# Gated recurrence of a two-layer block: outputs with tokens on partitions, chunk matmuls in column groups, norm along the free axis, scan between the state updates, one table set for exp and ln

## What is computed

```python
f = lb + (1.0 - lb) * jax.nn.sigmoid(f_x)
q = heads(jax.nn.silu(q_x)); k = heads(1.0 - f); log_f = heads(jnp.log(f)); v = heads(i_x)
b = jnp.cumsum(log_f, axis=3)                       # inside a chunk
q_rel = q * jnp.exp(b - b_ref); k_rel = k * jnp.exp(b_ref - b)
a = jnp.where(causal, q_rel @ k_rel.T, 0.0); o_intra = a @ v
q_dec = q * jnp.exp(b); k_dec = k * jnp.exp(b_last - b)
o_inter = q_dec @ state                             # per chunk
state = exp(b_last)[..., None] * state + k_dec.T @ v
o = rms_norm(o_intra + o_inter, o_norm) * silu(g_x) # norm over the 128 values
return o @ w_o
```

## Time and profile before

| | us |
|---|---|
| median of 3 runs | 1766.31 |
| lowest, highest | 1765.16, 1770.31 |
| span of the profiled execution, first to last instruction | 1764.1 |
| median less that span | 2.2 |
| recurrence, from the first score matmul of head 0 to that of head 7 | 1103.60 to 1312.89 |

### The profile page before, as it was taken

How to read it: one execution, slowest core, us unless ns; L and a number is a source line. 1 busy time by engine, 2 the same in 40 slices (tenths; PEclk the granted TensorE clock), 3 DMA queues, 4 the chain that set the end, 5 groups by cost and what they waited for, 6 DMA issues and landing times.

```text
span 1764.1 us, 28709 instructions
## 1 busy us (share of the span) xinstructions
PE 1648.9 (93%) x10394; PEld 1339.2 (76%) x10394; DVE 843.9 (48%) x1461; ACT 750.5 (43%) x1160; POOL 647.9 (37%) x374
## 2 busy tenths in 40 slices
PE   5999989988889999999999999899999999999996
PEld 4787668856666668878888887788878878888885
DVE  6555768856765645522121245565663532111125
ACT  2333334343744445524142347676764622223231
POOL 4454310004421125634444454233334544444440
PEclk9999999989899999999999999899999999999997
DMA  8622210003111123232333332122222223333331
GB/s 287 203 84 72 72 37 4 4 18 86 53 48 34 30 70 84 84 95 84 104 88 106 91 101 60 48 61 70 71 77 82 57 85 95 96 94 99 92 104 52
DMA packets 250959, 140.35 MB, mean 80 GB/s; under 512 B 10121, under 2 KB 242656, under 8 KB 250864
## 3 DMA queue, kind: packets, MB, share of 16 engines
q1 hardware_dynamic: 249552, 137.12, 26.7%
q0 software_dynamic: 1008, 1.66, 0.3%
q10 hardware_dynamic: 304, 0.26, 0.0%
HBM read 136.93 MB, written 2.10 MB: 79 GB/s over the span
## 4 chain that ended last, share of the span: by engine, by line
issue 40%; PE 24%; POOL 11%; DVE 11%; ACT 5%; DVEq 4%; DMA 2%; ACTq 1%; POOLq 1%; SPq 1%
PE bank L746 13%; POOL w_low L555 10%; DVE hg_state L2062 2%; DVE bank L2059 2%; PE bank L797 2%; PE bank L1035 1%; DVEq L2489 1%; DMA x_tok<-in_x 1%; DVE hg_k_dec L2059 1%; PE bank L1197 1%; PE bank L1196 1%; PE bank L1224 1%; DVEq L2802 1%; SPq L439 1%; ACTq L2008 1%
## 5 line engine op out<-in xcount | busy, mean ns | idle before, releaser
L555 POOL TENSOR_TENSOR w_low<-w_raw,w_high 128x1024 fp32r<-128x1024 f32 (+2 forms) x218 | 516.6, 2370 | 971.5 <-ACT w_high L1486 971.4
L746 PE MATMUL bank<-act_high,w_high 128*128 128x512 f32 x976 | 391.5, 401 | 12.3 <-POOL w_low L555 8.3
L746 PE MATMUL bank<-act_low,w_high 128*128 128x512 f32 x976 | 382.4, 392 | 0.0
L746 PE MATMUL bank<-act_high,w_low 128*128 128x512 f32 x976 | 382.2, 392 | 0.0
L1486 ACT ACTIVATE w_high<-w_raw 128x1024 fp32r<-128x1024 f32 (+2 forms) x218 | 219.1, 1006 | 282.2 <-PE bank L746 269.7
L746 PEld LDWEIGHTS bank<-act_high,w_high 128*128 128x128 f32 x976 | 184.0, 189 | 65.3 <-issue 12.2
L746 PEld LDWEIGHTS bank<-act_high,w_low 128*128 128x128 f32 x976 | 184.0, 189 | 40.1
L746 PEld LDWEIGHTS bank<-act_low,w_high 128*128 128x128 f32 x976 | 183.9, 188 | 38.8 <-issue 2.4
L746 PE MATMUL bank<-hid_high,w_high 128*128 128x512 f32 x472 | 185.1, 392 | 3.8 <-DVE mix_out L2731 3.8
L746 PE MATMUL bank<-hid_low,w_high 128*128 128x512 f32 x472 | 184.4, 391 | 0.0
L746 PE MATMUL bank<-hid_high,w_low 128*128 128x512 f32 x472 | 184.2, 390 | 0.0
(11 more groups left out here) (568 smaller groups left out, 2855.4 us busy)
## 6 DMA issues: line engine op xcount, KB each, us to landing
w_raw<-in_mlp_w SPq DMA_DIRECT2D x128, 512.0 KB, 4.0
w_raw<-in_hgrn_w_in SPq DMA_DIRECT2D x32, 512.0 KB, 4.1
w_raw<-in_w_in SPq DMA_DIRECT2D x29, 512.0 KB, 4.0
w_ada_piece<-in_w_ada SPq DMA_DIRECT2D x5, 2048.0 KB, 16.4
w_raw<-in_w_out SPq DMA_DIRECT2D x8, 512.0 KB, 3.9
w_raw<-in_mla_w_o SPq DMA_DIRECT2D x8, 512.0 KB, 3.9
w_raw<-in_hgrn_w_o SPq DMA_DIRECT2D x8, 512.0 KB, 3.9
w_raw<-in_mla_w_in SPq DMA_DIRECT2D x6, 512.0 KB, 4.0
```

Of the source, the lines that this page charges most:

```text
L555: gp.tensor_tensor(WL[:, c0 % 2, 0:kt, 0:m], WR[:, c0 % 2, 0:kt, 0:m], WH[:, c0 % 2, 0:kt, 0:m].bitcast(F32), ALU.subtract).then_inc(w_lo, 1)
L746: mm = pe.matmul(bank[0:m, :], w[:, k, 0:m], a[:, k0 + k, :], start=(k == 0 and n_ == 0), stop=(k == kt - 1 and n_ == 2))
```

## The change

PE makes the outputs with tokens on partitions: for each block of 128 tokens the masked scores are the weights and the values move (one full 128x128 matmul), and each chunk's 32 columns of q_dec are weights of one column group of the array, with its state moving, so that four chunks go to four groups of 32 output partitions. The sum of squares by a matmul is gone: ACT squares each 128x128 block with a sum along the free axis, takes Ln and Exp of 128x4 numbers, DVE scales each token's row and PE turns the result back (`turn_outputs`). The outputs stand after job G0+2 instead of before it (in the second call, after block 4 of job G0+3). DVE makes three state updates, then the scan, the differences and `scaled(1)`, then the other twelve. On ACT the gate's Silu moves beside that of q, one table set for exp and ln is loaded by hand, and q_dec's and the decay's exponential come behind the norm, ahead of `high(G0+4)`. The q_dec product waits for a semaphore of its own (`g_dec`).

```diff
@@ tensor
+                    else:
+                        pe.wait_ge(g_fin, o)
                     for c_ in range(NC - 1):
 ...
+                def outputs():
+                    pe.wait_ge(g_qdec, o + 1)
                     for t in range(TT):
-                        pe.matmul(PB[6][:, t * P:(t + 1) * P], VG[:, t, :], AT[:, t, :], start=True, stop=False)
+                        pe.matmul(PB[6][:, t * P:(t + 1) * P], AT[:, t, :], VG[:, t, :], start=(t == 0), stop=False)
                         for b in range(P // HC):
                             c_ = t * (P // HC) + b
                             if c_:
                                 pe.wait_ge(g_st, o * (NC - 1) + c_)
-                                mm = pe.matmul(PB[6][:, c_ * HC:(c_ + 1) * HC], ST[:, c_, :],
-                                               QDEC[:, c_ * HC:(c_ + 1) * HC], start=False,
+                                mm = pe.matmul(PB[6][b * HC:(b + 1) * HC, t * P:(t + 1) * P],
+                                               QDEC[:, c_ * HC:(c_ + 1) * HC], ST[:, c_, :], start=False,
 ...
-                def square_sum():
-                    pe.wait_ge(g_sq, o + 1)
-                    pe.matmul(PB[7][:, :], ONES[:, :], OSQ[:, :], start=True, stop=True).then_inc(g_ss, 1)
+                def turn_outputs():
+                    pe.wait_ge(g_scaled, o + 1)
+                    for t in range(TT):
+                        mm = pe.transpose(PB[5][:, t * P:(t + 1) * P], OTK[:, t, :], IDENT[:, :])
+                    mm.then_inc(g_back, 1)
                 if second:
-                    job(G0 + 3, n * 4, free["g"], n * 4 + 4, amid=square_sum)
+                    job(G0 + 3, n * 4, free["g"], n * 4 + 4, amid=outputs, amid_at=4)
+                elif o is not None and n is not None:
+                    job(G0 + 1, n * 4, free["g"], n * 4 + 2)
+                    job(G0 + 2, n * 4, free["g"], n * 4 + 3)
+                    outputs()
+                    job(G0 + 3, n * 4, free["g"], n * 4 + 4)
                 elif o is not None:
+                    part(W0, (free["go"], 1), "hgrn_o", 3, 7, HH, HL)
+                    outputs()
+                    part(W0 + 1, (free["go"], 2), "hgrn_o", 0, 4, HH, HL)
+                if o is not None:
+                    turn_outputs()
+                if n is not None and o is not None:
+                    turn_values(n, o)
@@ scalar
+                if o is not None:
+                    act.wait_ge(free["g"], o * 4 + 6)
+                    act.activation(GG[:, :], TG[3][:, :], ACT.Silu).then_inc(g_gate, 1)
 ...
+                act.preload_act_table_set("natural_log_exp_and_others")
                 if n is not None:
                     act.wait_ge(g_diff, n + 1)
 ...
                     act.activation(KDEC[:, :], TG[0][:, :], ACT.Exp)
+                    act.drain()
+                    act.sem_inc(g_exp, 1)
+                if o is not None:
+                    act.wait_ge(g_out, o + 1)
+                    for t in range(TT):
+                        act.activation(OSQ[:, t * P:(t + 1) * P], PB[6][:, t * P:(t + 1) * P], ACT.Square,
+                                       accum_out=OST[:, 0, t:t + 1])
+                    act.drain()
+                    act.activation(OST[:, 1, :], OST[:, 0, :], ACT.Ln, scale=1.0 / P, bias=CST[:, 3:4])
+                    act.drain()
+                    act.activation(OST[:, 2, :], OST[:, 1, :], ACT.Exp, scale=-0.5).then_inc(g_rstd, 1)
+                if n is not None:
                     act.activation(QDEC[:, :], BG[:, :], ACT.Exp)
 ...
                 if n is not None and o is not None:
                     high(G0 + 4, n * 4)
@@ vector
+                BEFORE = 3
+                if o is not None:
+                    states(0, BEFORE)
                 if n is not None:
                     dve.wait_ge(g_ln, n + 1)
                     dve.tensor_tensor_scan(BG[:, :], HRST[:, :], TG[2][:, :], 0.0, MUL, ADD)
 ...
+                if o is not None:
+                    states(BEFORE, T // HC - 1)
 ...
                 if o is not None:
-                    dve.wait_ge(g_sd, o + 1)
-                    stt(OG[:, :], OG[:, :], col("o_norm"), OSD[:, :], MUL, MUL)
+                    dve.wait_ge(g_rstd, o + 1)
+                    tt(OTK[:, :, :], PB[6][:, :].rearrange("p (t d) -> p t d", d=P), bc(OST[:, 2, :], P), MUL)\
+                        .then_inc(g_scaled, 1)
+                if n is not None:
+                    dve.wait_ge(g_dec, n + 1)
+                    tt(QDEC[:, :], QDEC[:, :], QG[:, :], MUL).then_inc(g_qdec, 1)
+                if o is not None:
                     dve.wait_ge(g_gate, o + 1)
-                    tt(OG[:, :], OG[:, :], GG[:, :], MUL)
+                    if n is not None:
+                        scaled(3, TG[3])
+                    dve.wait_ge(g_back, o + 1)
+                    stt(OG[:, :], PB[5][:, :], col("o_norm"), GG[:, :], MUL, MUL)
                     after(g_fin)
```

More of the change, by code:

```diff
@@ L1396, in hgrn @@
                     mm.then_inc(g_out, 1)
-                if n is not None:
-                    if o is not None and not second:
-                        job(G0 + 2, n * 4, free["g"], n * 4 + 3)
-                else:
-                    part(W0 + 1, (free["go"], 2), "hgrn_o", 0, 2, HH, HL)
-                def square_sum():
-                    pe.wait_ge(g_sq, o + 1)
-                    pe.matmul(PB[7][:, :], ONES[:, :], OSQ[:, :], start=True, stop=True).then_inc(g_ss, 1)
-                if second:
-                    job(G0 + 3, n * 4, free["g"], n * 4 + 4, amid=square_sum)
-                elif o is not None:
-                    square_sum()
@@ L1410, in hgrn @@
-                if n is None:
-                    part(W0 + 1, (free["go"], 2), "hgrn_o", 2, 4, HH, HL)
-                if n is not None:
-                    if o is not None:
-                        if not second:
-                            job(G0 + 3, n * 4, free["g"], n * 4 + 4)
-                        pe.wait_ge(g_sd, o + 1)
-                        turn_values(n, o)
+                def turn_outputs():
[3 more added lines that the diff above has]
+                    mm.then_inc(g_back, 1)
@@ L2008, in hgrn @@
                     act.drain()
-                    act.sem_inc(g_exp, 1)
+                    act.sem_inc(g_dec, 1)
                 if n is not None and o is not None:
                     high(G0 + 4, n * 4)
-                if n is None:
-                    act.activation(SMALL[:, 44:45], CST[:, 3:4], ACT.Ln)
-                if o is not None:
-                    act.wait_ge(g_ss, o + 1)
-                    act.activation(OSD[:, :], PB[7][:, :], ACT.Ln, scale=1.0 / P, bias=CST[:, 3:4])
-                    act.drain()
-                    act.activation(OSD[:, :], OSD[:, :], ACT.Exp, scale=-0.5).then_inc(g_sd, 1)
-                    act.wait_ge(free["g"], o * 4 + 6)
-                    act.activation(GG[:, :], TG[3][:, :], ACT.Silu).then_inc(g_gate, 1)
                 if n is not None:
@@ L2785, in hgrn, with states @@
                     dve.tensor_scalar(KG[:, :], FG[:, :], -1.0, 1.0, MUL, ADD)
-                if o is not None:
-                    if not second:
-                        low_of_output(o - 1)
-                    dve.wait_ge(g_inc, o + 1)
-                    for k in range(T // HC - 1):
+                if o is not None and not second:
+                    low_of_output(o - 1)
+                def states(k0, k1):
+                    for k in range(k0, k1):
                         ps = PB[2 + k % (P // HC)][:, k // (P // HC) * P:(k // (P // HC) + 1) * P]
                         if k == 0:
+                            dve.wait_ge(g_inc, o + 1)
                             dve.tensor_copy(ST[:, 1, :], ps).then_inc(g_st, 1)
```

46 lines of the change are left out of this document (17 added, 29 removed).

## The result

| | before | after |
|---|---|---|
| median of the runs on one chip | 1767.84 (1765.16 to 1770.31, 4 runs) | 1754.18 (1750.96 to 1758.42, 4 runs) |
| span of the profiled execution | 1764.1 | 1754.3 |
| one pass of the loop, score matmul to score matmul | 30.49 | 28.48 |

The ratio is 0.992, with a 95% interval of 0.990 to 0.994: 13.7 us, or 0.8%, faster. The same two kernels on another chip gave 1753.16 (5 runs) against 1772.68 (11 runs), a ratio of 0.989 (0.986 to 0.992). The forecast was 1755.2, between 1746 and 1765.

A forecast was written before the change was run, and what follows sets the result against it. PE's issued work (28.6) and a loop through ACT and POOL (28.7) were taken to bound a pass, down from 30.49. Six passes save 10.6 and the last call 0.5, 11.1 in all: 1766.3 to 1755.2, range 1746 to 1765.

The forecast's parts named there:

- PE's own work of 28.6 in a pass: In one pass of the loop, the matmul work PE issues was to sum to 28.6 us, against 30.5 before.
- The after-effect of the matmul with ones: On PE, removing the sum of squares was to save 0.46 plus 0.62 in job G0+3 behind it, 1.08 us.
- The chain over ACT and POOL: From the end of the outputs through norm and next head's weights to job G0: 7.86 us.
- the two bounds within 0.1: In the loop, PE's own work (28.6) and the loop through ACT and POOL (28.7) were taken as equal to 0.1 us.
- four squares with a sum ... 0.65 each: On ACT behind the outputs, four squares with read-outs were to take 2.60 us; lower end 1.2.
- The rival of a longer chain: ACT and POOL take longer between outputs and job G0: pass 29.8, time 1762; chance 0.16.
- I take 0 for the second call ... and -0.5 for the last: Outside the loop: no change in the second call (-1.8 to +1.8), 0.5 us saved in the last (-2 to +1).
- Both signs of being wrong: In the profile after: PE standing before `turn_outputs`, or waiting over one us before job G0.
- The states hidden with one us in hand: DVE's last state update was to end at 20.3, before PE's fourth output block needs it at about 21.4.
- The table loads "count at nothing": On ACT, loads fall from seven to four per pass, worth nothing since ACT has over 8 us idle.
- No overlap of the column groups (1774): In the outputs, narrow passes still cost 0.11 each plus mode changes: pass 31.3, time 1774; chance 0.08.
- No mode cost (1746): In the outputs, narrow groups follow full matmuls without a gap: outputs 1.8, pass 27.4, time 1746; chance 0.12.

The follow-up runs named there:

- the dummy: The changed kernel with one 128x512 fp32 matmul with ones put back ahead of job G0+3, result unread: 1755.74, ratio 0.993 to the kernel before.
- the scores-first version: The changed kernel with a head's four full score matmuls all ahead of the 15 narrow state matmuls: 1747.22, ratio 0.987 to the kernel before.
- the twin: The changed kernel with scores first, one wait for all states, then narrow matmuls round the column groups: 1755.57, ratio 0.991 to the kernel before.

## Why the prediction was right, and where it was not

The time came out 1.0 from the forecast, but that is partly luck: the forecast gain was 11.1 us, the medians say 13.7 (10.6 to 17.5 by the ratio's interval) and the stage in the traces 15.4. The likeliest case was the one that happened. By its steps:

- **PE's own work of 28.6 in a pass: right.** It is 28.48 in five of the six passes. Outputs 2.98 (forecast 3.1, bounds 2.9 to 3.3), a block 0.78 (0.73 to 0.85), job G0+3 5.61 behind the outputs (two jobs in a row are 11.01 with 11.02 forecast), scores and keys 1.25 (1.31), turning back 0.43 (0.36). The narrow pass in bursts of eight, two for each of the four groups, is (0.43 - 0.27)/7 = 0.023 (forecast 0.031).
- **The after-effect of the matmul with ones: right in kind.** 1.08 were forecast, 0.83 came back with the dummy. The difference is mostly the wait for the values at the end of job G0+3, which the dummy doesn't bring back.
- **The chain over ACT and POOL "7.86", so "the two bounds within 0.1": this step failed in its size.** It takes 6.35 and has 1.38 to spare. The mis-sized term is "four squares with a sum ... 0.65 each": they are 0.26 apart, 1.22 in all instead of 2.60. The 0.65 was read off, an exponential with a bias vector, and in the other pair of rows the large copy `w_high_s` behind the read-out, and the 0.30 behind the read-out was taken for the read-out's own cost. The lower end that stood beside it, 1.2, was the value. The pass would have been the same within 0.2 either way, which is why the forecast survived. The rival of a longer chain falls with it for five of the six passes. Its mechanism is real, though: it lengthens the first pass by 1.47, which the forecast took to be like the others, and when two table loads or a late scan use up the slack, PE waits exactly where the rival said.
- **"I take 0 for the second call ... and -0.5 for the last": mis-sized, and most of what the forecast missed.** They are -1.95 and -1.86, 3.3 more than forecast. In the second call PE does meet a long wait, but it stands ahead of the outputs, for the weights, and behind it the outputs run with no wait at all. Before, PE waited in small parts in between, for states and `scaled`, worked for 9.63 us at the lower clock, and at the end waited 2.66 for the values. The forecast priced no clock at all, and of the 1.95 its share isn't separated. In the last call, 1.21 of waiting for DVE went too, which no term had. The other 1.0 is in the loop: 11.6 over six passes (1.48 + 10.1) where 10.6 was forecast. Both signs of being wrong that the prediction named for PE's waits did show, if outside the five passes: PE stands 0.35 before `turn_outputs` in the second call and 1.22 before job G0 in the first pass.
- **The states hidden with one us in hand: right.** 0.76 (21.65 less 20.9). It is this margin that the scores-first version uses up: its narrow passes take 0.28 more than the twin's that waits for no state in between.
- **The table loads "count at nothing": in the old order no run tests it, in the new order it is wrong.** Two loads in the norm would cost 1.28 a pass, since the norm now stands ahead of the next head's weights on ACT. The load placed by hand is what keeps the forecast of the pass true.
- **No overlap of the column groups (1774): out.** A narrow pass costs 0.11 in its own group and 0.028 round the groups. The rival's price holds: by the estimate above it adds 2.3 to a pass of 28.48, which makes 30.8 where the prediction had 31.3, more than before the change.
- **No mode cost (1746): out,** as three pairs of changes are worth 0.74, or 0.99 without the wait for states. The Trainium skill's rule that a change of mode drains the engine ("TensorEngine Tiling (Array Packing)", Key Properties) agrees.

Still open: what sets the 0.11 of a pass, narrow or full, and how much of the second call's gain is the clock's.

## What to carry to other kernels

Where one engine is busy for the whole loop, count its work from start to start and then put a number on the slack of every chain that runs beside it; here 1.38 us of slack decided whether two table loads and the place of the scan cost anything. When small and full matmuls alternate, sort them so that the array changes its mode once, and let neighbouring narrow matmuls use different column groups. A mean over a row of many passes can hide that half of them overlap, so look at single passes before calling one cheap. The calls ahead of and behind a pipelined loop have waits of their own, so price them from their own rows: 3.3 of the 4.3 us that the forecast missed in this stage lay there, and so did 2.7 us of further gain. A wait there can cost more than its length: behind one of 7.16 us 15 matmuls took 5.51 instead of 3.54, since the clock was at its lower level for most of them.

## What the runs showed of the hardware that was not expected

- A Square of 128x128 from PSUM with a sum repeats every 0.26 us, its read-out included.
- Fp32 passes follow each other after 0.11 us within one column group (32 columns of weights, 128 that move), and full passes do so too, with 128 or with 32 columns that move. Four column groups run side by side: 0.028 for a pass round the groups, 0.023 in bursts of eight.
- A job's second 128x512 matmul starts 0.63 behind the first if an fp32 128x512 matmul stands before it, 0.34 behind narrow passes and 0.31 behind transposes (1194.37 to 1194.68 in the pass above).
- The granted clock in the 590 us ahead of the changed stage differs from run to run with identical instructions (1.00, 0.99, 0.98), and the length of that stretch by up to 7.7 us, half of what the change is worth.
- Behind a wait of 7.16 us the granted clock was 0.61 over 15 matmuls of 128x512, and they took 5.51 us; behind one of 1.33 it was 1.00, and they took 3.54.
